# Cross-attention of a two-layer step: when the sample scores, the sample softmax, the keys' turn and the cached-value products run

## The reference, cut to what matters

```python
def mem_kv(mem, g_mem, w_k, w_v):
    m = rms_norm(mem, g_mem)
    return (m @ w_k).reshape(b, 256, 4, 256), (m @ w_v).reshape(b, 256, 4, 256)

def cross_attend(h, k, v, w_q, w_o):          # h: 512 prompt rows, or 8 sample rows
    q = (h @ w_q).reshape(b, length, 4, 256)
    s = einsum('blhd,bmhd->bhlm', q, k) * 256 ** -0.5
    p = softmax(s, axis=-1)
    return einsum('bhlm,bmhd->blhd', p, v).reshape(b, length, 1024) @ w_o
```

## Time and profile before

| | |
|---|---|
| three executions | 2998.2, 2985.1, 2995.2 us; median 2995.2 |
| profiled execution, its span | 2991.2 us, 2989.1 us |
| PE busy | 2754.0 us, 92% |
| DVE, ACT busy | 1356.5 us (45%), 872.2 us (29%) |
| attention stage, layer 0 | 926.1 to 1025.3 us |
| attention stage, layer 1 | 2449.6 to 2544.7 us |

### The profile page before, as it was taken

One profiled execution on the slowest core, in us unless ns is written; L12 is line 12 of the kernel. 1 busy time (PEld: TensorE's weight loads), 2 busy tenths in 40 slices (PEclk: granted clock), 3 DMA queues, 4 the chain that ended last, 5 costly groups with the idle time before them and its releaser, 6 DMA issues.

```text
span 2989.1 us, 49821 instructions
## 1 busy us (share of the span) xinstructions
PE 2754.0 (92%) x21418; PEld 2640.2 (88%) x21418; DVE 1356.5 (45%) x2102; ACT 872.2 (29%) x1053; POOL 202.7 (7%) x164
## 2 busy tenths in 40 slices
PE   7999999776987899999999999999787988999999
PEld 7999999655886699999999999998766875999998
DVE  5444233214466244443344424676566472444422
ACT  4332221221323233322222222443222332333322
POOL 2000000001100010000000000004210010100001
PEclk9999999875988999999999999999897999999999
DMA  4333323004246233332233333222122392233331
GB/s 122 91 91 103 91 74 92 28 8 127 79 154 205 71 89 92 91 106 88 78 91 91 107 88 77 57 66 77 35 68 85 105 291 85 72 93 91 100 95 57
DMA packets 472039, 277.43 MB, mean 93 GB/s; under 512 B 24753, under 2 KB 460722, under 8 KB 471875
## 3 DMA queue, kind: packets, MB, share of 16 engines
q1 hardware_dynamic: 462844, 242.00, 28.5%
q0 software_dynamic: 8704, 33.56, 3.2%
q10 hardware_dynamic: 370, 0.13, 0.0%
HBM read 258.16 MB, written 17.68 MB: 92 GB/s over the span
## 4 chain that ended last, share of the span: by engine, by line
PE 86%; DVE 6%; ACT 3%; issue 2%; POOL 1%; DMA 1%; ACTq 0%; SPq 0%; DVEq 0%; POOLq 0%
PE ACC L443 24%; PE ACC L445 24%; PE ACC L444 24%; PE ACC L1097 2%; PE M L1887 1%; PE M L1378 1%; POOL keep L2473 1%; PE M L1421 1%; PE ACC L1887 1%; ACT w_hi L526 1%; PE M L1818 0%; DVE w_lo L532 0%; PE ACC L2017 0%; PE M L1124 0%; PE M L1083 0%
## 5 line engine op out<-in xcount | busy, mean ns | idle before, releaser
L443 PE MATMUL ACC<-xg_hi,w_hi 128*128 128x260 f32 x3968 | 1131.2, 285 | 27.2 <-DVE gp L713 14.8
L445 PE MATMUL ACC<-xg_hi,w_lo 128*128 128x260 f32 x3968 | 1126.5, 284 | 0.0
L444 PE MATMUL ACC<-xg_lo,w_hi 128*128 128x260 f32 x3968 | 1122.9, 283 | 0.0
L532 DVE TENSOR_TENSOR w_lo<-raw,w_hi 128x1024 fp32r<-128x1024 f32 (+1 forms) x330 | 426.7, 1293 | 1005.6 <-ACT w_hi L526 1005.4
L443 PEld LDWEIGHTS ACC<-xg_hi,w_hi 128*128 128x128 f32 x3968 | 753.4, 190 | 28.3 <-DVE w_lo L532 15.0
L444 PEld LDWEIGHTS ACC<-xg_lo,w_hi 128*128 128x128 f32 x3968 | 752.3, 190 | 0.0
L445 PEld LDWEIGHTS ACC<-xg_hi,w_lo 128*128 128x128 f32 x3968 | 752.0, 190 | 0.0
L526 ACT ACTIVATE w_hi<-raw 128x1024 fp32r<-128x1024 f32 (+1 forms) x330 | 368.0, 1115 | 1196.5 <-PE ACC L445 1196.5
L444 PE MATMUL ACC<-hid_lo,w_hi 128*128 128x260 f32 x1408 | 398.3, 283 | 0.0
L445 PE MATMUL ACC<-hid_hi,w_lo 128*128 128x260 f32 x1408 | 397.6, 282 | 0.0
L443 PE MATMUL ACC<-hid_hi,w_hi 128*128 128x260 f32 x1408 | 397.4, 282 | 0.0
(11 more groups left out here) (547 smaller groups left out, 3406.2 us busy)
## 6 DMA issues: line engine op xcount, KB each, us to landing
raw<-in_ffn_w_gate SPq DMA_DIRECT2D x88, 512.0 KB, 3.9
raw<-in_ffn_w_up SPq DMA_DIRECT2D x88, 512.0 KB, 3.8
raw<-in_ffn_w_down SPq DMA_DIRECT2D x64, 704.0 KB, 4.6
cache<-in_cache_mem_k POOLq DMA_DIRECT2D x16, 1024.0 KB, 6.3
cache<-in_cache_mem_v POOLq DMA_DIRECT2D x16, 1024.0 KB, 5.5
raw<-in_gd_w_in SPq DMA_DIRECT2D x32, 512.0 KB, 4.1
raw<-in_ml_w_in SPq DMA_DIRECT2D x24, 512.0 KB, 3.9
raw<-in_xa_w_q SPq DMA_DIRECT2D x16, 512.0 KB, 4.4
```

The lines of the kernel that those rows point to most:

```text
L443: pe.matmul(out, wh, hi[:, k0 + k, m], start=begin, stop=False)
L444: pe.matmul(out, wh, lo[:, k0 + k, m], start=False, stop=False)
L445: mm = pe.matmul(out, wl, hi[:, k0 + k, m], start=False, stop=end)
L532: dve.tensor_tensor(w_lo[:, j % 2, 0:n], raw[:, (j + d) % 4, 0:n], w_hi[:, j % 2, 0:n].bitcast(F32), ALU.subtract).then_inc(w_split, 1)
```

## The change

- The memory is scaled after ACT's step of query unit 2 instead of 3; `memg_hi` follows unit 4 instead of 5, `memg_lo` unit 5 instead of 6.
- `by_token` runs inside key unit 1 instead of ahead of it. The eight spreads stand ahead of the consecutive key units 3 to 7 and value units 0 to 2, instead of ahead of every second unit, and so do the scores on DVE.
- The keys' turn back (kvN 0 and 1) runs inside value units 1 and 2, into the two ACC banks that these phases leave free; `sT` inside value unit 3, `pT8` inside value unit 6, and the sample softmax between them on DVE and ACT, behind their steps 3 to 6.
- After the last value unit: scores of head 0, the values' turn, products of samples 0 and 1, scores of head 1, and in each head the products stand between `t` and `o`: sample 2, samples 3 and 4, samples 5 and 6, sample 7. Before, two products stood behind each head.
- `vN` is stored from two copies; `yl` of the last head moves behind `yl8`, and unit 0 of the output phase waits for it inside.

No instruction is added on PE; ACT has a few more, since the copies are smaller.

The diff, cut to its core:

```diff
@@ at_pe, at_dve: the order of the steps that are waited for (cut) @@
+        VAL = [[0, 1], [2], [3, 4], [5, 6], [7]]
@@ act_mem, dve_mem @@
-            return {1: squares, 3: scaled, 5: high}
+            return {1: squares, 2: scaled, 4: high}
-            return {1: mean, 4: to_sbuf, 6: low}
+            return {1: mean, 4: to_sbuf, 5: low}
@@ pe_kv_natural(pe, l, n), one turn a call @@
+            src = kT if n < 2 else vT
+            if n == 0:
+                pe.wait_ge(acc_free, XA[l][1].t0 + KC)
+            elif n == 1:
+                at_act.wait(pe, "kvN", 0, r=l)
+            elif n == 2:
+                pe.wait_ge(acc_free, XA[l][2].t0 + KC)
+                at_dve.wait(pe, "sc", NS - 1, r=l)
+            else:
+                at_act.wait(pe, "e8", r=l)
+        def natural(n):
+            return [ACC[:, 1:4:2, :], ACC[:, 1:4:2, :], M[:, 2:4, :], ACC[:, 0:2, :]][n]
@@ pe_queries @@
+            def sample_turned():
+                at_dve.wait(pe, "sc", NS - 1, r=l)
+                at_act.wait(pe, "kvN", 1, r=l)
+                for m in range(MT):
+                    mm = pe.transpose(ACC[0:32, 1, m * P:(m + 1) * P], sc[:, m * 32:(m + 1) * 32], ident[:])
+                at_pe.done(mm, "sT")
+            def sample_probs():
+                at_dve.wait(pe, "pn8", r=l)
+                ...
-            k = {1: by_token, 2: lambda: spread(0), 4: lambda: spread(1), 6: lambda: spread(2)}
-            v = {0: lambda: spread(3), 2: lambda: spread(4), 4: lambda: spread(5), 6: lambda: spread(6)}
-            return k, v, lambda: spread(7)
+            k = {3 + b: lambda b=b: spread(b) for b in range(5)}
+            v = {0: lambda: spread(5), 1: lambda: spread(6), 2: lambda: spread(7)}
+            k_mid = {1: by_token}
+            v_mid = {1: lambda: pe_kv_natural(pe, l, 0), 2: lambda: pe_kv_natural(pe, l, 1), 3: sample_turned, 6: sample_probs}
@@ pe_attn @@
-            at_act.wait(pe, "vst", r=l)
-            at_dve.wait(pe, "vlo", 1, r=l)
+            at_dve.wait(pe, "klo", r=l)
+            at_dve.wait(pe, "sc", NS - 2, r=l)
             scores(0)
+            pe_kv_natural(pe, l, 2)
+            pe_kv_natural(pe, l, 3)
+            at_dve.wait(pe, "pT8", r=l)
+            for b in VAL[0]:
+                values(b)
             scores(1)
             for h in range(XH):
+                if h == 0:
+                    at_act.wait(pe, "vst", r=l)
                 ...
                 at_pe.done(mm, "t", h)
+                for b in VAL[h + 1]:
+                    values(b)
                 at_dve.wait(pe, "pl", h, r=l)
                 ...
-                values(2 * h)
-                values(2 * h + 1)
@@ dve_scores @@
+            def bound():
+                dve_k_low(dve, l)
+                at_pe.wait(dve, "sT", r=l)
+                own.link(dve.tensor_reduce(st8, ACC[0:32, 1, 0:NMEM], AX.X, ALU.max))
+                at_dve.done(dve.tensor_scalar(nb8, st8, -SCALE, None, ALU.mult), "nb8")
+            k = {1: by_token}
+            k.update({3 + b: lambda b=b: sample_scores(b) for b in range(5)})
+            v = {b: lambda b=b: sample_scores(5 + b) for b in range(3)}
+            v.update({3: bound, 5: probs, 6: spaced})
@@ act_attention @@
-            act_phase(act, phs[2], after={1: lambda: act_k_high(act, l, phs)})
-            act_kv_natural(act, l)
+            act_phase(act, phs[2], after={0: lambda: act_k_high(act, l, phs), 1: lambda: act_k_natural(act, l, 0),
+                                          2: lambda: act_k_natural(act, l, 1), 4: lambda: act_sample_exps(act, l)})
```

More of the change, by code:

```diff
@@ L1014, in pe_mem @@
             at_pe.done(mm, "memT")
[L1016 to L1038, removed]
+        def pe_kv_natural(pe, l, n):
+            src = kT if n < 2 else vT
[8 more added lines that the diff above has]
+                at_act.wait(pe, "e8", r=l)
+            to = natural(n)
+            for c in range(KC):
+                mm = pe.transpose(to[:, c // 4, (c % 4) * P:(c % 4 + 1) * P], src[:, c, (n % 2) * P:(n % 2 + 1) * P], ident[:])
+            at_pe.done(mm, "kvN", n)
@@ new lines, in natural, with act_k_natural, act_v_high @@
+        def natural(n):
+            return [ACC[:, 1:4:2, :], ACC[:, 1:4:2, :], M[:, 2:4, :], ACC[:, 0:2, :]][n]
+        def act_k_natural(act, l, n):
+            at_pe.wait(act, "kvN", n, r=l)
+            for b in range(2):
+                ins = act.activation(kN[:, n, b * 512:(b + 1) * 512], ACC[:, 1 + 2 * b, :], ACT.Copy)
+            at_act.done(ins, "kvN", n)
+        def act_v_high(act, l, n):
+            at_pe.wait(act, "kvN", n, r=l)
+            at_act.done(act.activation(vN_hi[:, n - 2, :].rearrange("p (b c) -> p b c", b=2), natural(n), ACT.Copy), "kvN", n)
@@ L1043, in act_k_high, with dve_k_low @@
             at_act.done(act.activation(kT_hi[:], kT[:], ACT.Copy), "khi")
-        def dve_kv_low(dve, l):
+        def dve_k_low(dve, l):
             at_act.wait(dve, "khi", r=l)
             at_dve.done(dve.tensor_tensor(kT_lo[:], kT[:], kT_hi[:].bitcast(F32), ALU.subtract), "klo")
[L1048 to L1051, removed]
         SCALE = float(XD) ** -0.5
@@ L1208, in bound, with normed @@
                 at_dve.done(dve.tensor_scalar(nb4, st4, -SCALE, None, ALU.mult), "nb", h)
[L1209 to L1213, removed]
+            def normed(h):
                 at_act.wait(dve, "e", h, r=l)
@@ L1216, in dve_attn @@
                 at_dve.done(dve.tensor_tensor(pr[:], pr[:], rd4.unsqueeze(2).to_broadcast([P, TB, NMEM]), ALU.mult), "pn", h)
[L1217 to L1222, removed]
+            bound(0)
+            dve_v_low(dve, l, 0)
+            normed(0)
+            dve_v_low(dve, l, 1)
+            bound(1)
+            for h in range(XH):
+                if h > 0:
+                    normed(h)
+                    if h < XH - 1:
+                        bound(h + 1)
                 at_act.wait(dve, "pT", h, r=l)
                 at_dve.done(dve.tensor_tensor(prT_lo[:], ACC[:, 0:2, :], prT_hi[:].bitcast(F32), ALU.subtract), "pl", h)
[L1225 to L1231, removed]
-                lo(h)
+                if h < XH - 1:
+                    lo(h)
             at_pe.wait(dve, "pv", NS - 1, r=l)
```

84 lines of the change are left out of this document (49 added, 35 removed).

## The result

The changed kernel takes 2962.5 us (median of 4 runs, 2956.5 to 2969.6), the kernel before 2996.3 beside it (4 runs, 2985.1 to 2998.2): a ratio of 0.990 (0.986 to 0.993). Forecast were 2955 us and a gain of 36.3 us; the medians lie 33.8 apart. The profiled execution is the slowest of the changed kernel's four: 2969.6 us, its span 2967.7, which is 21.4 us under the span before.

A forecast was written before the change was run, and what follows sets the result against it. PE, busy 92% of the span, was taken as the bound, with its waits and the low clock after them to be cut. Gains of 22.3 and 14.0 us, together 36.3 off 2991.2, gave 2955 us, range 2940 to 2974.

The forecast's parts named there:

- (a): Query phase: memory scaled one unit earlier, so PE finds it ready for its turn; net gain 5.8 and 4.2 us.
- (b): First key unit to the end of the fourth: 2.2 us wait replaced by 3.1; gain 1.9 us, loss 1.1.
- (c): Twelve other key and value units: eight consecutive score units ask DVE for too much; 55.5 us, loss 17.1 and 16.7.
- (d): Attention stage: waits for scores, stored values, exponentials and splits go or are covered; 67.5 us, gain 31.7 and 27.6.
- One of the forecast's own signs of being wrong: Score units' clock under 0.9; others: twelve units under 48 or over 65 us, DVE cache-slot waits, attention stage over 75.
- the low clock: PE at 1.2 GHz after gaps, a low microsecond losing about 0.45 us; in the twelve units 2.4 us.
- the wait for score 7: Value unit 3: PE reaches `sT` at 34.3 us and waits 3.8 us for the last sample's scores.
- the rival in which the clock falls in the score units: PE idles 1 us in each score unit and the clock is low throughout: 22 us, so 2977; chance 0.15.
- the wait for `q40`: First four key units: PE has done the third at 9.5 us, DVE makes `q40` by 12.6; wait 3.1 us.
- The rival of the transfers: Score units: loads of 1.57 MB a unit set the pace, slower than before; 3009 us at 200 GB/s; chance 0.05.
- The table load: Sample exponentials on ACT: 1.28 us without a drain; by the skill's page `pn8` would come 1.4 us later a layer.

The follow-up runs named there:

- the holes made even: The changed kernel with four more matmuls of 512 columns (result unused) ahead of spread 1 only; ratio 0.987 (0.984 to 0.990).

## Why the prediction was right, and which term was mis-sized

Its terms, gains negative, in us for layers 0 and 1:

| term | predicted | measured |
|---|---|---|
| (a) memory, last query units | -5.8, -4.2 | -6.3, -4.9 |
| (b) first four key units | -1.9, +1.1 | -0.4, +2.3 |
| (c) twelve units | +17.1, +16.7 | +20.9, +23.0 |
| (d) attention stage | -31.7, -27.6 | -31.3, -27.2 |
| output projection | 0, 0 | -1.4, 0.0 |
| rest of the span | 0 | +3.9 |

The layers sum to gains of 18.5 and 6.8 us, the span to 21.4. The rest of the span lies outside both attentions, where no instruction changed. So the traced gain is 15 us short of the 36.3 forecast, 11 of them inside the attentions. That the medians lie 33.8 apart, within 3 us of the forecast, is therefore partly luck. One of the forecast's own signs of being wrong also came true: the clock in the score units is under 0.9, with 5.6 us at 1.00 and 5.2 at 0.67 in turn, and over the twelve units it is 0.88 and 0.83.

(a) and (d) came out within 0.7 us each, and by the waits and the work that were told. The stage was forecast at 67.5 and is 67.9, with the waits of 0.9, 0.9 and 3.8 that the text counted (5.5 in all) and 0.9 at the end where it had 1.2. The two kernels that move products show that (d) is no luck: the stage changes by the waits that they cover and the clock behind those.

The mis-sized term is the low clock. In (c) the forecast put PE's waits ahead of the spreads at 5.8 us; they are 5.7. It put the wait for score 7 at 3.8; it is 3.8. It put 2.2 to 2.6 at value unit 6; it is 1.2. What it had at 2.4 us, the low clock, is 7.5 and some 10: what is left of 59.3 and 61.7 without 40.9 of work and 10.9 of waits. A pair of units takes 10.8 us where 9.1 was worked out. Forecast was an alternation of 1.3 and 0.6; what came is 1.9 and nothing. The two are coupled. Where the clock falls after 1.9 us of idling, the next unit runs at 0.67 and is so long that DVE is done when it ends, so the wait after it is nothing, the next unit runs at full clock and is too short, and 1.9 us come again. Where the clock does not fall, the waits are 0.5 and 1.3 in turn and the pair 9.2, as forecast; the same score units did this in two layers of other kernels. With the holes made even, and with matmuls in the holes, pairs are at 9.2 as well. So the rival in which the clock falls in the score units was half true: it had all eight units at 0.50 and 22 us, what came is three of a layer at 0.51 to 0.72, some 12 us over the forecast's 2.4 a layer in both together. Forecast and rival were put as excluding each other; the truth is that either rhythm can come, and this execution had the slower one in both layers.

In (b) the wait for `q40` is 3.1 us, as worked out, and the low clock behind it costs 1.2 to 1.5 us more than the 1.9 taken, by the stretches' excess over 18.0. This too differs between executions: behind the same wait the next unit ran at 0.50 or 0.54 in the changed kernel, at 0.50 to 0.67 in the others but for one at 1.00.

The rival of the transfers is false as told: with half of DVE's work the same loads ran faster. Its grain of truth is the start of the key phase, where four loads of 1 MB let go at once hold up the weights. It costs the changed kernel nothing, for the wait for `q40` covers it; with that wait gone it cost some 5 us a layer, the wait and the low clock of the unit with it.

The table load, in the timeline of ACT in the changed kernel:

```profile
930.15 1.06 ACT L526 ACTIVATE w_hi<-raw 128x1024 fp32r<-128x1024 f32 x1 [3.25 <-PE ACC L445]
931.23 1.28 ACT L1180 ACT_TABLE_LOAD   x1
932.52 0.46 ACT L1180 ACTIVATE keep<-ACC,tmp 32x256 f32<-32x256 f32 x1
```

The load starts 0.02 us after the work before it and the exponential right at its end: 1.28 us and no drain beside. The 1.38 us of the Trainium skill (ScalarE: Activation LUTs, What ACT_TABLE_LOAD costs) are not seen, and the wait that they would have lengthened, at value unit 6, came out 1 us shorter than forecast, not longer.

What stays open: the low clock is tied to the long waits, but not every long wait brings it, and what decides between the two rhythms no run shows. And the 34 us between the medians are more than the 21 us between the two profiled executions; the changed kernel's profiled execution is its slowest, and where its other three gained 4 to 13 us no profile shows. Fewer falls of the clock in the score units, worth 1.6 us a pair, could be a part of it; that is an estimate from the two rhythms.

## What to carry to other kernels

Where one engine feeds another with a little too much work per unit, count not only the waits but how long each single one is: two waits of 0.9 us cost their length, one of 1.9 mostly costs the clock of the unit behind it too. Put a step that waits for another engine one unit later where its result is not needed yet: here that took 3.8 us of wait to 0.7. Before you credit an edit with a change of rhythm, look whether other executions of the same instructions have that rhythm too. And when a wait is taken away, look for what started late under its cover, here the weights behind a burst of loads.

## What the runs showed that was not expected

- The clock goes with how idle time is cut. At the same 3.66 us of PE work a unit, waits of 0.9 us in every unit of 4.6 leave the granted clock at 1.00 throughout; waits of 1.9 us ahead of every second mostly bring 0.67 in the unit that follows, which costs 1.5 us. Counted over the timelines of the changed kernel and its ten variants, waits for scores ahead of a spread: of 39 up to 1.02 us none was followed by a unit under 1.00, of 6 between 1.2 and 1.3 three were, of 31 between 1.6 and 2.0 it was 26 (0.51 to 0.72), of 4 between 2.3 and 3.3 two. The length of the wait makes the fall likely; it does not decide it alone. The Trainium skill (TensorE: Matmul & The Clock Gate, A second HAM failure mode) tells of small idles that make the clock swing; here the larger ones mostly did, and the smaller, twice as frequent ones did not.
- Four loads of 1 MB, let go together on one queue, held up half a megabyte of weights on another so that ACT waited 7.7 us for them, at 284 to 287 GB/s over the key and value units; spread out, they moved at 312 and 323 GB/s, and ACT did not wait for key or value weights. With the loads let go together the weights were late in six layers of six in this order of steps, with the loads apart in none of two.
